# Exponentials in a written-out step of the first table pass, and four PSUM banks for its tiles' sums

## What is computed

```
q = (xc @ w_q).reshape(T, PEER_HEADS, 2, PEER_QDIM // 2)
s = einsum('thcd,hcnd->thcn', q, sub_keys)
sv, si = top_k(s, 16)                       # per head and half
comb = sv[:, :, 0, :, None] + sv[:, :, 1, None, :]
cv, ci = top_k(comb, 16)                    # 16 experts per token and head
w = softmax(cv)
a = gelu(einsum('td,thkd->thk', xc, u_tab[eidx])) * w
y = einsum('thk,thkd->td', a, v_tab[eidx])
```

## Time and profile before

| | us |
|---|---|
| median of 3 runs | 2953.02 |
| lowest, highest | 2951.01, 2953.2 |
| profiled execution, its own time | 2951.89 |
| its span, first to last instruction | 2950.2 |
| tiles 0 to 87 of the first pass, layer 0 | about 1102 to 1366 |
| tiles 88 to 127, layer 0 | about 1366 to 1513 |
| tiles 0 to 87, layer 1 | about 2167 to 2431 |

### The profile page before, as it was taken

The page is one execution under the profiler, slowest core; times in us unless marked ns, Lnnn a source line. Parts: engine busy times, 40 slices in busy tenths (PEclk is TensorE's granted clock), DMA queues, the critical chain, the costliest instruction groups (busy, mean ns, idle before and its releaser), DMA issues.

```text
span 2950.2 us, 51661 instructions
## 1 busy us (share of the span) xinstructions
PE 2817.8 (96%) x17556; PEld 2517.7 (85%) x17556; DVE 1989.1 (67%) x3725; ACT 1482.9 (50%) x2397; POOL 489.1 (17%) x390
## 2 busy tenths in 40 slices
PE   8889998999999989999999999999899999999998
PEld 6679887788789889999988888785899999988886
DVE  4557975679965759866866666516479848766666
ACT  2444454544443444667855555205245668745554
POOL 0000100011100000477700000000000787400000
PEclk9999999999999999999999999989999999999999
DMA  8638973489854445666556666540355775566663
GB/s 283 209 116 260 346 252 112 128 243 355 331 171 129 143 143 177 176 174 157 137 178 215 214 215 213 126 143 15 93 176 178 178 174 135 145 212 216 215 213 131
DMA packets 355204, 547.85 MB, mean 186 GB/s; under 512 B 71073, under 2 KB 251681, under 8 KB 354466
## 3 DMA queue, kind: packets, MB, share of 16 engines
q1 hardware_dynamic: 303618, 471.46, 50.3%
q0 software_dynamic: 51488, 75.11, 9.8%
HBM read 545.33 MB, written 15.84 MB: 190 GB/s over the span
## 4 chain that ended last, share of the span: by engine, by line
PE 90%; DVE 4%; ACT 3%; DMA 2%; issue 1%; ACTq 0%; SPq 0%; DVEq 0%
PE ps L1002 34%; PE ps L929 12%; PE ps L933 12%; PE ps L930 12%; PE ps L980 4%; PE ps L1369 2%; DMA tile_ring<-mlp_w_in 1%; PE ps L1490 1%; PE ps L904 1%; PE ps L1132 1%; PE ps L863 1%; PE ps L1579 1%; PE ps L874 1%; PE ps L964 1%; PE ps L1030 1%
## 5 line engine op out<-in xcount | busy, mean ns | idle before, releaser
L929 PE MATMUL ps<-x_high,w_high 128*128 128x256 f32 x3264 | 819.2, 288 | 28.5 <-DVE x_low L2730 10.6
L930 PE MATMUL ps<-x_low,w_high 128*128 128x256 f32 x3264 | 805.1, 284 | 0.0
L929 PEld LDWEIGHTS ps<-x_high,w_high 128*128 128x128 f32 x3264 | 628.5, 193 | 41.3 <-issue 26.0
L800 POOL DMA_INDIRECT by_key<-spare x256 | 420.1, 1641 | 1330.3 <-DVE spare L2805 1216.0
L930 PEld LDWEIGHTS ps<-x_low,w_high 128*128 128x128 f32 x3264 | 629.8, 193 | 0.4
L2231 DVE TENSOR_TENSOR w_low<-tile_ring,w_high 128x1024 fp32r<-128x1024 f32 x256 | 313.8, 1226 | 249.4 <-ACT w_high L1821 249.4
L933 PE MATMUL ps<-x_high,w_low 128*128 128x256 f32 x3264 | 460.8, 284 | 1.4 <-DVE w_low L3026 1.4
L1821 ACT ACTIVATE w_high<-tile_ring 128x1024 fp32r<-128x1024 f32 x256 | 271.5, 1061 | 346.0 <-PE ps L1002 346.0
L933 PEld LDWEIGHTS ps<-x_high,w_low 128*128 128x128 f32 x3264 | 423.9, 193 | 1.6 <-DVE w_low L3026 1.6
L1002 PE MATMUL ps<-w_high,x_high 128*128 128x512 f32 x1440 | 389.9, 393 | 21.2 <-DVE x_low L2186 16.7
L1964 ACT ACTIVATE w_high<-tile_ring 128x1024 fp32r<-128x1024 f32 x256 | 270.7, 1058 | 262.9 <-PE ps L933 215.5
(11 more groups left out here) (365 smaller groups left out, 3253.2 us busy)
## 6 DMA issues: line engine op xcount, KB each, us to landing
tile_ring<-peer_u SPq DMA_DIRECT2D x256, 512.0 KB
tile_ring<-peer_v SPq DMA_DIRECT2D x256, 512.0 KB
arena<-mod_w POOLq DMA_DIRECT2D x112, 512.0 KB, 6.4
tile_ring<-mlp_w_in SPq DMA_DIRECT2D x64, 512.0 KB
tile_ring<-mlp_w_out SPq DMA_DIRECT2D x64, 512.0 KB
tile_ring<-ret_w_in SPq DMA_DIRECT2D x48, 512.0 KB
tile_ring<-peer_w_q SPq DMA_DIRECT2D x32, 512.0 KB
by_key<-zero_rows POOLq DMA_DIRECT2D x16, 896.0 KB, 5.1
```

What stands on the lines that cost most here:

```text
L800: pool.indirect_dma_start(out=flat, out_offset=bass.IndirectOffsetOnAxis(ap=slot_at[0:SCATTER, n:n + 1], axis=0), in_=slot_weight[0:SCATTE ...
L929: nc.tensor.matmul(dst, cols, x_high[:, c, :], start=c == 0, stop=False)
L930: nc.tensor.matmul(dst, cols, x_low[:, c, :], start=False, stop=False)
```

## The change

The exponential moves four tiles ahead (32 and 64 in place of 36 and 68). It no longer stands between two loops: the four tiles 32 to 35 (and 64 to 67) are written out behind the loop, and the exponential stands behind the first `high` of that step. Tiles' sums rotate over banks 4 to 7, and PE waits for the gelu of tile k-4, not k-2; the first four tiles of layer 0 don't wait at all. `finish(b)` on DVE moves along, to behind low(34) and low(66).

```diff
--- before.py
+++ after.py
@@ -50,7 +50,7 @@
 LOTS = (T - SCATTER) // HOT
 WEIGH_FROM = P - RING - LOTS
 ACT_ROWS = (3, 2)
-RAISED_AT = (36, 68)
+RAISED_AT = (32, 64)
 HULL = 4 * TOPK + (TOPK - 4) * 4
 PANEL = 2048
 CLEAR = 16
@@ -1354,11 +1354,10 @@
                 u0 = UNITS[f"weigh{l}"]
 
                 def tile(j, k, begun=True):
-                    a = k % 2
-                    if begun or k >= 2:
-                        pe.wait_ge(gate_stored, j * RING + (t0 + k - 1))
+                    if begun:
+                        pe.wait_ge(gate_stored, j * RING + (t0 + k - RING + 1))
                     at = j * RING + (n0 + k + 1)
-                    column_products(ps[:, 4 + a, 0:T], a, (high_ready, at), (low_ready, at)).then_inc(act_sums, 1)
+                    column_products(ps[:, 4 + k % RING, 0:T], k % 2, (high_ready, at), (low_ready, at)).then_inc(act_sums, 1)
 
                 def four_tokens(j, g):
                     u = u0 + g
@@ -1965,16 +1964,18 @@
 
                 def gelu(k, j):
                     act.wait_ge(act_sums, j * RING + (t0 + k + 1))
-                    A(gates[:, j * RING + k, :], ps[:, 4 + k % 2, 0:T], ACT.Gelu_apprx_tanh).then_inc(gate_stored, 1)
+                    A(gates[:, j * RING + k, :], ps[:, 4 + k % RING, 0:T], ACT.Gelu_apprx_tanh).then_inc(gate_stored, 1)
 
                 def gelu_apart(k, j):
                     act.wait_ge(act_sums, j * RING + (t0 + k + 1))
                     act.wait_ge(gate_merged, j * RING + (m0 + k - WEIGH_FROM - 1))
-                    A(raised[k % 2], ps[:, 4 + k % 2, 0:T], ACT.Gelu_apprx_tanh).then_inc(gate_stored, 1)
-
-                def tiles(j):
+                    A(raised[k % 2], ps[:, 4 + k % RING, 0:T], ACT.Gelu_apprx_tanh).then_inc(gate_stored, 1)
+
+                def tiles(j, raise_block=None):
                     for k in range(RING):
                         high(k + 2, j)
+                        if k == 0 and raise_block:
+                            raise_block()
                         gelu(k, j)
 
                 def rows_of(j, g):
@@ -2011,9 +2012,12 @@
                 for b in range(TB):
                     with act.Fori(j0, RAISED_AT[b] // RING) as j:
                         tiles(j)
-                    act.wait_ge(routed, TB * l + b + 1)
-                    A(route[:, b, 2, :], route[:, b, 2, :], ACT.Exp).then_inc(pick_exp, 1)
-                    j0 = RAISED_AT[b] // RING
+
+                    def raise_block():
+                        act.wait_ge(routed, TB * l + b + 1)
+                        A(route[:, b, 2, :], route[:, b, 2, :], ACT.Exp).then_inc(pick_exp, 1)
+                    tiles(RAISED_AT[b] // RING, raise_block)
+                    j0 = RAISED_AT[b] // RING + 1
                 with act.Fori(j0, WEIGH_FROM // RING) as j:
                     tiles(j)
                 act.wait_ge(unit_taken, u0)
```

## The result

| | before | changed |
|---|---|---|
| median (5 runs each) | 2951.01 us | 2936.61 us |
| lowest, highest | 2949.69, 2953.2 | 2932.8, 2938.89 |
| span of the profiled execution | 2950.2 | 2934.9 |

The ratio is 0.9948 (95% interval 0.9933 to 0.9962): the changed kernel is 0.5% faster. The forecast was faster by 13.3 us, to 2939.5 with a range of 2936.8 to 2943.5. The direction held; the time lies 0.2 us under the range.

A forecast was written before the change was run, and what follows sets the result against it. PE bounds the kernel, losing 6.78 us per layer waiting on gelu banks. Gain 13.5 less 0.2 for the tie is 13.3 us, giving 2938.6 or 2939.7, named 2939.5; range 2936.8 to 2943.5.

The forecast's parts named there:

- both causes are hit twice: In the later loops and at the exponentials: loops without table loads, and four banks, remove PE's waits; at most 13.5 us.
- t0: Start of ACT's rounding of tile 34, from which the prediction timed the written-out step.
- a tie with PE: At tile 35 of each written-out step: PE could start at t0 + 5.48, wanted 5.44; cost 0.05 four times, 0.2 us.
- The table switches: On ACT around each exponential: a switch costs 1.30 us; by the skill's rule 2.66, making tile 35 2.7 us late.
- 0.14 in the bound: Upper bound of the gain in both layers' passes: 2 x 6.78 = 13.56, taken as 13.5 us.
- All else keeps its length: Sign expected in the profile after: everything apart from the listed changes in the pass keeps its length.
- the runs' own spread of 2 us: Part of the 8-in-10 range, 2936.8 to 2943.5, beside the forecast and most of the lost tie.
- Behind tile 87: Stretch after tile 87: nothing to gain, since PE is busy 133.1 of 134 us.
- The tie was not lost: Rival: rounding of tile 35 comes later than computed and PE waits in four places; 2941.5 to 2946.3, chance 0.10.
- No switch was longer: Rival: a drain of about 1.38 us appears at each of two switches per step; 2950.4, chance 0.02.
- Code loading on ACT: Rival: written-out steps wait for new code; 1.9 us each gives 2947.3, chance 0.03; 4.6 us gives 2976, 0.02.
- Nothing else held PE in the loops: Rival: something else, such as the rounding or tiles' loads, holds PE in the loops; 2946, chance 0.05.

The follow-up runs named there:

- The added copies: Changed kernel with one or two more 128x128 copies on ACT behind each exponential: passes 251.49 us with one, 251.89 and 251.88 with two.
- the step alone: Changed kernel with the two banks of before, keeping the written-out step with the exponentials at tiles 32 and 64: 2946.5 us, ratio 0.9985.

## Why the prediction was right and where it failed

**Right.** PE was the bound, and the loss was 1.69 us at each exponential and 0.30 in each pass of the later loops. Its sum was 6.78 a layer and it measured 6.84 and 6.80. The cause was the bank of the tile two back, as the prediction said; the four banks alone give all of it. Its "both causes are hit twice" held as well: without loads in the loops, 5.6 us of it come back with two banks. The written-out step is not needed beside the banks.

**The new step.** It foretold the rounding of tile 35 at t0 + 4.29 and measured 4.28. It foretold a tie with PE, 0.04 us late, and took 0.05 for it, four times. There was no loss: the rounding of tile 34 came 0.06 us later than the usual distance (2.94 for 2.88), and PE started 0.05 behind the end of the rounding of tile 35, not 0.13. This term was 0.2 and measured 0. The added copies show that the room is 0.02 at most.

**The table switches.** The rows of the changed kernel show 1.29 and 1.30 us from the start of a load to that of its activation, and 0.02 from the end of an activation to a load. The Trainium skill (ScalarE: Activation LUTs, "What ACT_TABLE_LOAD costs") has a drain on top of each load, 2.66 us a switch, by which, as an estimate, the two switches would have been 2.7 us longer; no drain shows in the changed kernel either.

**DVE.** `finish(0)` waited for the exponential, as foretold, and `w_low` of tile 35 waited 0.28 us for its rounding behind it, at 1200.49 where the prediction's working puts it (t0 + 5.36):

```profile
1197.85 0.29 DVE L2803 TENSOR_REDUCE small<-route 128x8 f32<-128x128 f32 x1 [0.40 <-ACT route L2018]
...
1200.49 1.23 DVE L2795 TENSOR_TENSOR w_low<-tile_ring,w_high 128x1024 fp32r<-128x1024 f32 x1 [0.28 <-ACT w_high L1963]
...
1202.95 1.21 DVE L2795 TENSOR_TENSOR w_low<-tile_ring,w_high 128x1024 fp32r<-128x1024 f32 x1
```

`w_low` of tile 36 follows 2.46 us later, and PE did not wait.

**Where it failed.** The forecast was "against the median" 2953.02 - 13.3 = 2939.7, named as 2939.5, and the mean of the changed kernel is 2936.0. Of the 3.7 us between 2939.7 and 2936.0 the passes account for 0.34: 13.64 measured for 13.3, by the tie's 0.2 and by 0.14 in the bound. Two larger terms were wrong. The level: 2953.02 was the median of three executions and the mean over 54 is 2951.7, so it was 1.3 us too high. And "All else keeps its length", a term of nothing: the rest of the program came out 2.0 us shorter on the mean, and moved by 11 us between traces of the kernel before alone.

The step that failed is the one that was to take this in, the range with "the runs' own spread of 2 us". Three executions showed 2.2 us between the lowest and the highest; 54 of them showed 13.2 (2945.8 to 2959.0), with a standard deviation of 2.8. A range of 2.7 below the forecast could hold neither that spread nor the two wrong terms. The mechanism and the size of the gain in the passes were right; the range was built on three runs as if they showed the spread. The median came out 0.2 us outside it, and one so near its edge could as well have come out inside, by chance.

**Behind tile 87.** The prediction found nothing to gain there, since PE is busy 133.1 of 134 us. The missing 0.9 are one wait, at the stage's first one-hot rows. In the kernel before:

```profile
1366.95 1.15 PE L1369 MATMUL ps<-spread,route 128*128 128x128 f32 x8 [0.90 <-ACT spread L1990]
```

The version that makes these rows ahead gained 1.16 us in each layer. A busy share near 1 over a long stretch still hid a wait worth removing.

**The rivals.** The tie was not lost. No switch was longer. Code loading on ACT didn't appear: the step's first load stands 0.02 us behind the rounding. Nothing else held PE in the loops.

## What to carry to other kernels

A slow instruction on a helper engine costs only what it holds back: ask what waits for it, and whether one more buffer there takes it off the path. Before a loop is entered, let the table stand that its body needs, since the build can't know it at the loop's head and then loads it in every pass; a single small activation in front of the loop was enough here. And measure a change of some microseconds by the distance between two fixed instructions in the traces, which came out the same to 0.05 us here where the whole time moved by 13.

## What the runs showed of the hardware

A wait of PE of 1.73 us was followed, 1.3 us after it ended, by 3.4 us at the lower clock level and cost 1.49 us more than the wait. This came in both traces of the step alone at one of four equal waits, at the same one. Waits of 1.43 us were never followed by it, in 24. The wait of 2.27 us at the head of the second table pass, the same in both layers of all 18 traces, was followed by it in 29 cases of 36, and not in layer 1 of the two traces in which the drop had come in the pass before. So the length of the wait alone doesn't decide. Copies of 0.29 us placed between two other activations put the next one off by 0.19 only. What lies outside the two passes moved by up to 11 us between executions of one program, and ahead of the first pass it moved with the time at the lower clock level.
